# Streaming encoder step: seven-product block matmuls in all four feed-forwards, with sums formed in PSUM and three additions a tile on GpSimd

## What is computed

```python
def conv_ffn(h, hist, w_up, w_conv, b_conv, w_down):
    a, gate = jnp.split(h @ w_up, 2, axis=-1)          # D_FF = 2816 each
    ext = jnp.concatenate([hist.astype(a.dtype), a], axis=1)
    conv = b_conv
    for j in range(CONV_W):                            # 3 taps over time
        conv = conv + ext[:, j:j + t] * w_conv[j]
    return (jax.nn.silu(conv) * gate) @ w_down, ext[:, t:]
```

## Time and profile before

| | us |
|---|---|
| median of the 3 runs | 3951.88 |
| the 3 runs | 3951.88, 3933.93, 3956.92 |
| span of the profiled execution | 3929.5 |
| PE busy | 3692.2 (94%) |
| DVE busy | 2321.4 (59%) |
| ACT busy | 1128.6 (29%) |
| POOL busy | 758.1 (19%) |

### The profile page before, as it was taken

The page is one execution under the profiler, slowest core; times in us unless marked ns, Lnnn a source line. Parts: engine busy times, 40 slices in busy tenths (PEclk is TensorE's granted clock), DMA queues, the critical chain, the costliest instruction groups (busy, mean ns, idle before and its releaser), DMA issues. The chain is left out here.

```text
span 3929.5 us, 54494 instructions
## 1 busy us (share of the span) xinstructions
PE 3692.2 (94%) x21676; PEld 2935.9 (75%) x21676; DVE 2321.4 (59%) x4713; ACT 1128.6 (29%) x2672; POOL 758.1 (19%) x812
## 2 busy tenths in 40 slices
PE   7997899999999999999999998999989999899998
PEld 5765577787877667778767787887766777688887
DVE  1664566498963664549556554488955565554542
ACT  1124333211124442321234332111134443322221
POOL 2300220301101232220100015312000101453334
PEclk9998899999999999999999999999999999999999
DMA  4331223412212222342312123343221212342223
GB/s 146 97 113 58 83 90 95 137 52 78 84 51 75 69 88 84 105 124 81 96 63 73 60 66 116 114 115 110 73 80 40 77 38 67 87 145 86 65 82 96
DMA packets 151606, 339.55 MB, mean 86 GB/s; under 512 B 30184, under 2 KB 68648, under 8 KB 138040
## 3 DMA queue, kind: packets, MB, share of 16 engines
q1 hardware_dynamic: 91576, 291.04, 23.7%
q10 hardware_dynamic: 59776, 45.02, 3.9%
HBM read 299.33 MB, written 36.68 MB: 86 GB/s over the span
## 5 line engine op out<-in xcount | busy, mean ns | idle before, releaser
L901 PE MATMUL PS<-xn,wring 128*128 128x272 f32 (+1 forms) x7168 | 1682.0, 394 | 33.9 <-DVE xn L1527 11.7
L901 PEld LDWEIGHTS PS<-xn,wring 128*128 128x128 f32 x7168 | 1374.8, 194 | 298.4 <-issue 37.4
L1859 POOL TENSOR_TENSOR xT<-xT,res 128x272 f32<-128x272 f32 (+1 forms) x320 | 253.9, 795 | 2302.9 <-ACT res L1184 2254.8
L901 PE MATMUL PS<-dense,wring 128*128 128x256 f32 (+1 forms) x2816 | 662.7, 394 | 11.9 <-DVE dense L1509 6.3
L901 PEld LDWEIGHTS PS<-dense,wring 128*128 128x128 f32 x2816 | 537.6, 194 | 111.5 <-issue 10.9
L1604 DVE MAX8 top<-scr 128x8 f32<-128x384 f32 (+6 forms) x418 | 367.4, 879 | 12.2
L1605 DVE MATCH_REPLACE8 scr<-top,scr 128x384 f32<-128x384 f32 (+6 forms) x418 | 359.9, 861 | 0.0
L1184 ACT ACTIVATE res<-PS 128x272 f32<-128x272 f32 (+1 forms) x320 | 123.2, 387 | 587.0 <-PE PS L901 565.4
L922 PE MATMUL PS<-wring,xn 128*128 128x256 f32 (+1 forms) x1152 | 267.9, 392 | 4.0 <-ACT dense L1198 4.0
L922 PEld LDWEIGHTS PS<-wring,xn 128*128 128x128 f32 (+1 forms) x1152 | 213.1, 187 | 53.6 <-issue 8.8
L901 PE MATMUL PS<-catT,wring 128*128 128x272 f32 (+1 forms) x1024 | 231.5, 387 | 5.3 <-issue 2.7
(11 more groups left out here) (199 smaller groups left out, 4113.2 us busy)
## 6 DMA issues: line engine op xcount, KB each, us to landing
wring<-in_wu SPq DMA_DIRECT2D x88, 1024.0 KB, 4.9
wring<-in_wf SPq DMA_DIRECT2D x88, 512.0 KB, 3.7
wring<-in_wo SPq DMA_DIRECT2D x64, 512.0 KB, 3.7
wring<-in_wd SPq DMA_DIRECT2D x96, 320.0 KB, 2.9
wring<-in_wd SPq DMA_DIRECT2D x64, 384.0 KB, 3.1
wring<-in_wn SPq DMA_DIRECT2D x16, 1024.0 KB, 5.3
kv<-out_projT ACTq DMA_DIRECT2D x48, 256.0 KB, 4.1
out_projT<-dense SPq DMA_DIRECT2D x40, 272.0 KB
```

Source lines behind the costliest of these rows:

```text
L901: mm = nc.tensor.matmul(PS[:, dbank(t.g0), 0:cw], wtile(t.q, i), rhs, start=(kk == a), stop=(kk == b - 1))
L1859: nc.gpsimd.tensor_tensor(x, x, res[:, i % NRES, 0:cw], ALU.add).then_inc(s_res, 1)
```

## The change

All four feed-forwards get seven-product tiles, for n from 1 to 21 (84 tiles instead of 20). The products come in another order (P5 before P7). P6 is accumulated onto P1 in the same bank after ACT has copied P1 out, P7 onto that, P4 onto that, and P3 onto P5. So four of the seven additions a tile fall away; the three that are left go from DVE to POOL. The convolution still waits for the sum of branch a's second group, now POOL's third addition. T2 to T4 and the partial results get buffers of their own (`xsum`, `parts`); T1 overwrites B12 in `xn`. The unused code that put the other half of `xT` aside goes, and so do the table `bmask` and its load. The down projection's parts become 7, 7, 4 and 4 tiles, run after tiles 7 and 14 and, the last two together, after tile 21. `tanh_turn` is as before: for a seven-product tile the tanh comes three turns after the tile's last product.

```diff
-PARTS = ((0, 6), (6, 12), (12, 17), (17, 22))
+PARTS = ((0, 7), (7, 14), (14, 18), (18, 22))
+UP_TO = (8, 15, 22, 22)
...
-SEVEN = {(1, 1): range(1, NF - 1)}
+SEVEN = {x: range(1, NF) for x in PROJS}
...
-PRODUCTS = (Product("P1", "A11", "B11"), Product("P2", "A12", "B21"), Product("P6", "S2", "T2"), Product("P7", "S3", "T3"),
-            Product("P5", "S1", "T1"), Product("P3", "S4", "B22"), Product("P4", "A22", "T4"))
+PRODUCTS = (Product("P1", "A11", "B11"), Product("P2", "A12", "B21"), Product("P6", "S2", "T2"), Product("P5", "S1", "T1"),
+            Product("P7", "S3", "T3"), Product("P3", "S4", "B22"), Product("P4", "A22", "T4"))
+GOES_ON = ("P6", "P7", "P4", "P3")
...
-U_ORDER = ("U2", "a0", "U3", "P5 + P3", "a1", "g0", "g1")
-
-ON_POOL = ()
+U_ORDER = ("a0", "g1", "a1")
...
-    for p, upto in enumerate((8, 14, 19, 22)):
-        for n in range(upto):
-            if n >= (0, 8, 14, 19)[p] and n in SEVEN.get((l, h), ()):
+    for p, upto in enumerate(UP_TO):
+        for n in range(UP_TO[p - 1] if p else 0, upto):
+            if n in SEVEN.get((l, h), ()):
...
+        xsum, parts = sb("xsum", [P, 3, 4 * GMAX]), sb("parts", [P, 3, GMAX])
...
-            if name in ("P6", "P7", "P3", "P4"):
+            if name in ("P2", "P7", "P3"):
                 lane.wait_ge(s_ea, t.g0 + 1)
-            if name == "P6":
-                eng.tensor_tensor(u2, u2, p1, ALU.add).then_inc(s_fix, 1)
-                into_a(c0, p1, 0)
+            if name == "P2":
+                into_a(c0, part_of(t, 0))
             elif name == "P7":
-                lane.wait_ge(s_fix, fixed + 1)
-                eng.tensor_tensor(u3, u3, u2, ALU.add).then_inc(s_fix, 1)
+                eng.tensor_tensor(g, g, part_of(t, 2), ALU.add).then_inc(s_fix, 1)
             elif name == "P3":
-                into_a(c1, g, c1)
-                lane.wait_ge(s_fix, fixed + 4)
-                into_a(c1, u2, 0)
-            elif name == "P4":
-                lane.wait_ge(s_fix, fixed + 4)
-                eng.tensor_tensor(g0, g0, u3, ALU.add).then_inc(s_fix, 1)
-                eng.tensor_tensor(g1, g1, u3, ALU.add).then_inc(s_fix, 1)
+                into_a(c1, part_of(t, 1))
...
-                        mm = nc.tensor.matmul(PS[:, dbank(t.g0), 0:cw], ws[:, P * i:P * i + P], xs[:, i, :], start=(i == 0), stop=(i == 3))
+                        mm = nc.tensor.matmul(PS[:, dbank(t.g0), 0:cw], ws[:, P * i:P * i + P], xs[:, i, :],
+                                              start=(i == 0 and x.name not in GOES_ON), stop=(i == 3), skip_group_check=x.name in GOES_ON)
...
-                        act.wait_ge(s_xs, 4 * list(SEVEN).index((t.l, t.h)) + 1)
-                        act.wait_ge(s_fix, max(0, len(U_ORDER) * (B - 1) + {"P1": 2, "P6": 5, "P7": 7}[name]))
+                        act.wait_ge(s_fix, max(0, len(U_ORDER) * (B - 1) + {"P1": 1, "P6": 3, "P7": 2}[name]))
...
-                if t.kind == "s" and (t.l, t.h) not in ON_POOL:
-                    add_products(dve, nc.vector, t)
...
                     if name == "P2":
                         pool.wait_ge(s_mm, t.g0 + 1)
                         weight_sum(BLOCK_Q[t.q], "S4", "A12", "S2", ALU.subtract)
-                    elif name == "P7" and next_block is not None:
+                    add_products(pool, nc.gpsimd, t)
+                    if name == "P7" and next_block is not None:
                         first_sums(next_block)
```

More of the change, by code:

```diff
@@ L194 @@
         FIRST_OF[_t.q] = _k
-ASIDE = [x for x in SEVEN if x in ((0, 1), (1, 0))]
-BACK = [x for x in SEVEN if x != (1, 1)]
 def group_of(block, name):
@@ L660, in x_block @@
             (c0, cw), (c1, _) = GRP[h]
-            if name in ("T2", "T3", "T4") or name == "T1" and (l, h) == (1, 1):
-                a = 4 * cw * (int(name[1]) - 2)
-                flat = scr[:, 0:4 * cw] if name == "T1" else x_all[1 - h][:, a:a + 4 * cw]
-                return flat.rearrange("p (k t) -> p k t", k=4)
+            if name in ("T2", "T3", "T4"):
+                return xsum[:, int(name[1]) - 2, 0:4 * cw].rearrange("p (k t) -> p k t", k=4)
             k, c = {"B11": (0, c0), "B12": (0, c1), "T1": (0, c1), "B21": (4, c0), "B22": (4, c1)}[name]
@@ L668, in part_of @@
         def part_of(t, i):
-            cw = GRP[t.h][0][1]
-            return x_all[1 - t.h][:, (12 + i) * cw:(13 + i) * cw]
+            return parts[:, i, 0:GRP[t.h][0][1]]
         def a_cols(t, c, cw):
@@ L1851, in pool_program @@
                     weight_sum(next_block, "S1", "A21", "A22", ALU.add)
-                if (t.kind, t.n, t.p, t.j) == ("wo", 0, 0, 0) and PROJS.index((t.l, t.h)):
-                    pool.wait_ge(s_back, 16 * sum(1 for x in BACK if x < (t.l, t.h)))
                 if t.kind in ("wo", "dn"):
```

53 lines of the change are left out of this document (12 added, 41 removed).

## The result

The changed kernel takes 4031.97 us (median of 4 runs, 4014.39 to 4039.85), the one before 3948.61 (4 runs, 3933.93 to 3956.92): a ratio of 1.0219, 95% interval 1.0182 to 1.0256. The prediction was 3929, with a range of 3859 to 4016: the sign is wrong, and the time lies outside the range. The profiled execution of the changed kernel took 4029.23 us, with a span of 4027.0; that of before had 3929.5.

What follows compares the result with a forecast made beforehand. PE was taken as the bound (busy 3692 of 3929.5 us), with DVE nearly full beside the selection. Savings of 5 + 35 + 1.7 less losses of 7 + 12 gave 22.7 us: 3951.9 to 3929 us, range 3859 to 4016.

Steps and rivals of the forecast that it cites:

- Step 1: Products of all new seven-product tiles: four matmuls fewer a tile, 114.7 us of PE time less.
- Step 2: 31 tiles beside the top-k selection, DVE nearly full: meetings with POOL cost 2 us a tile; 51 of 56 us go.
- Step 3: Other 32 tiles: the chain behind POOL's third addition makes each 0.7 us late; 22 of 57 us go.
- Step 4: F11: the same chain at 256 columns, 12.7 against 12.07 us a tile, costs 7 us.
- Step 5: Down projection's parts: POOL's pace in the last part and the two longer parts cost 12 us.
- GpSimd sets the pace: Rival, at the convolution: late tanh holds P6's copy and so P7; 50 us more, 4002 us, chance 0.28.

Runs made afterwards that it cites:

- e3: The changed kernel with the three additions a tile on GpSimd left out, the four weight sums kept: 3943 us, 1.0008 of the kernel before.
- e2: The changed kernel with GpSimd's four weight sums a tile left out, the three additions kept: 3916 us, 0.9934 of the kernel before.
- h13: The changed kernel without GpSimd's sums and additions, with P4's four matmuls done as eight, so 32 a tile: 4003 us, 1.0132 of the kernel before.
- e8: The changed kernel with the down projection's parts as before (6, 6, 5, 5 blocks, third part after tile 18): 4035 us, 1.0239 of the kernel before.
- e7: The changed kernel with both GpSimd's four weight sums and its three additions left out: 3890 us, 0.9869 of the kernel before.
- e4: The changed kernel with ACT's tanh, and DVE's product behind it, one turn later: 4046 us, 1.0264 of the kernel before.
- f9: The changed kernel with each GpSimd weight sum in four pieces of 128 columns instead of one of 512: 4026 us, 1.0234 of the kernel before.
- e6: The changed kernel with the three additions on VectorE (DVE) instead of GpSimd: 4027 us, 1.0215 of the kernel before.

## Why the prediction was wrong

**Step 1, the products: right.** L874 has 2688 records that read `xn` and 3 x 672 that read `xsum`, 4704 in all; 336 records of F11, six tiles, take 72.0 us as before.

**Step 2, DVE where it is nearly full: the price of a meeting was about right, what it was set against failed.** Meetings were put at 2 us a tile; the excess of F00, F01 and F10 grew by 85 us, 1.35 a tile (1.3 to 1.7 by the ways of counting above). But the step then compared DVE's load with PE's and let the stretch end with the fuller one: F01 and F10 level, F00 5 us better. From the start of the output projection to the first down part, 21 tiles in all, the three stages became 17.3, 16.5 and 11.8 us longer where 37.7 us of matmuls should have gone. That is a loss of 83 us, 4.0 a tile, where the step had 1.6 (51 us for 31 tiles). F00 up to tile 17, which was to stay near 405 us, is 39 us longer than before (14 of them for the two longer down parts). DVE is at 86 to 94% and PE at 85 to 92%, because both now wait in turn. And T1 to T4 were counted only as 6 us of DVE time, not by their place: T1 alone stopped PE for 9.49 us in F00 and 8.6 in F10.

**Step 3, the chain in the other 32 tiles: the failed step without a price for its main term.** It said 0.7 us a tile, from a chain without mixers. F01 from its first down part on grew by 32.7 us where 14 x 1.72 = 24 should have gone: 57 us, 4 us a tile. In the rest of F00 with P10 it is 3.4 us a tile, in the rest of F10 1.1. The step named the reason ("the DVE steps queued behind the wait come late, and so do the transposes that wait for them") and gave it no price, and it let ACT's copies have cover "while a mixer step is under 2 us", which counts such a step's length and not its wait for DVE. The 122.6 us of idle time ahead of the products are that term, for this step's tiles and step 2's together and T1's part apart. e3 and e2 show how it hangs on GpSimd: without the additions in the chain F01 is 41 us shorter, without the sums 43. And cover did not help as the step believed: in the stages with mixers a matmul taken away gave back only half its time (h13).

**The clock: no term at all.** Up to 61 us in the three stages. The rows of before gave a hint, not a rule: the later stretch of F01 and the one of F10, with 2.3% and 5% of idle time on PE, had 0.97 and 0.96, those of F00 and F11 1.00, but so had the earlier one of F01, which is idle for 2.3% as well.

**Step 4, F11: wrong, in the other direction.** The chain takes 11.6 us, not 12.7, against 12.1, so it costs 0 and not 7. Most of the difference lies in two places: from the end of S1 to the end of L1519 it took 0.7 us where step 3 had 1.2, and S4 came beside L1520, 8.9 us after P7's start, where step 3 had it behind that instruction, at 10.3.

**Step 5, the down parts: too high.** 12 us were expected, e8 shows none that can be measured. F11 as a whole is 2.4 us longer. Its end has GpSimd's last sum 8.28 us ahead of PE, before 7.40.

**The rivals.** "GpSimd sets the pace" came nearest (4002, still 30 us short), and e7 confirms that GpSimd's part is worth 138 us. Its mechanism, the tanh that holds P6's copy and so P7, is in the trace: PE's idle time ahead of P7, 43 us, goes to that copy, as the prediction had said it would. It is a third of the idle time ahead of the products, and e4 shows that moving the tanh does not free PE. The larger part stands behind mixer steps on ACT that wait for a late DVE, and those waits no rival had priced.

What stays open: how much of the loss is the clock and how much idle time, since no run could change one alone; whether the half that is lost of a matmul goes by short bank turns (C) or by missing cover (D); and the wait of ACT at L1250 in the selection stretches, for which no experiment was made.

## What to carry to other kernels

A matmul saved is worth its whole time where PE is busy without a gap, as in F11; in the stages where the mixers' chain runs beside it, it was worth half. Before moving work to an engine, look at what stands in order behind it on the engines that wait, and follow each wait over the second engine to the one that is late. Two causes can hide each other, so that each repair alone shows nothing (f9, e6) where both together give 49 us. When a change helps one stage and harms another, try it by stage: the version with seven products in the second layer only, additions on DVE and sums in pieces, is 1.0% faster than the kernel before.
